# Transposed activations with 260-element rows in place of 256, and the warm-up tile in the `wide` buffer

## The reference

```python
xn = rms_norm(x, pre_norm)                       # (256, 2048)
proj = xn @ w_in                                 # 25 chunks of 512 columns, and 12 of merge gates
ya = dilated_attention(rope(q), rope(k), v) * silu(gate_a)
yb = banded_window_attention(rope(q), rope(k), v, 128, sink) * silu(gate_b)
yc = hgrn2_bidirectional(c_q, f_fwd, f_bwd, c_i, c_gate, ...)
y = g0 * (ya @ w_branch_a) + g1 * (yb @ w_branch_b) + g2 * (yc @ w_branch_c)
x = x + rms_norm(y @ w_out, post_norm)
```

## Time and profile before

| | before |
|---|---|
| median of 3 runs | 2167.24 us (2167.20 to 2167.29) |
| profiled execution, first to last instruction | 2165.5 us |
| outside this span (median less span) | 1.8 us |
| PE busy | 2156.1 us (100%) |
| PEld busy (loads of the stationary operand) | 1806.1 us (83%) |
| DVE / ACT / POOL busy | 70% / 49% / 58% |
| matmuls, and loads | 10062 each |

### The profile page before, as it was taken

The page is one execution under the profiler, slowest core; times in us unless marked ns, Lnnn a source line. Parts: engine busy times, 40 slices in busy tenths (PEclk is TensorE's granted clock), DMA queues, the critical chain, the costliest instruction groups (busy, mean ns, idle before and its releaser), DMA issues.

```text
span 2165.5 us, 25788 instructions
## 1 busy us (share of the span) xinstructions
PE 2156.1 (100%) x10062; PEld 1806.1 (83%) x10062; DVE 1517.6 (70%) x2192; ACT 1062.6 (49%) x1040; POOL 1258.3 (58%) x583
## 2 busy tenths in 40 slices
PE   9999999999999999999999999999999999999998
PEld 8888888888888888888888888888888888888887
DVE  7872789888656785655388637898996566865653
ACT  6444344546556564434454434345466566544442
POOL 4455544436685767666544555444476857676664
PEclk9999999999999999999999999999999999999999
DMA  8555444444445444655565554454544444546554
GB/s 327 192 191 193 173 175 180 151 176 183 168 173 176 174 175 168 251 193 191 192 217 193 192 192 175 169 181 148 184 176 174 174 175 163 186 166 251 192 193 151
DMA packets 59752, 403.66 MB, mean 186 GB/s; under 512 B 6768, under 2 KB 6896, under 8 KB 12272
## 3 DMA queue, kind: packets, MB, share of 16 engines
q1 hardware_dynamic: 59488, 401.49, 51.1%
q10 hardware_dynamic: 144, 0.52, 0.1%
HBM read 397.80 MB, written 4.19 MB: 186 GB/s over the span
## 4 chain that ended last, share of the span: by engine, by line
PE 98%; DVE 1%; DMA 1%; issue 0%; ACT 0%; DVEq 0%; POOLq 0%; POOL 0%; ACTq 0%
PE acc L1260 91%; PE side L1260 7%; DMA raw<-w_stream 1%; DVE w_lo L470 0%; PE side L1427 0%; ACT w_hi L467 0%; PE side L412 0%; DVE wide L1020 0%; DVE arena L893 0%; DVEq L482 0%; ACT stage L633 0%; POOLq L482 0%; POOL small L616 0%; DVE warm L967 0%; DVE small L885 0%
## 5 line engine op out<-in xcount | busy, mean ns | idle before, releaser
L470 POOL TENSOR_TENSOR w_lo<-raw,w_hi 128x768 fp32r<-128x768 f32 x367 | 1035.5, 2822 | 866.7 <-ACT w_hi L467 855.8
L467 ACT ACTIVATE w_hi<-raw 128x2048 fp32r<-128x2048 f32 x366 | 701.1, 1916 | 957.5 <-PE acc L1260 929.8
L470 DVE TENSOR_TENSOR w_lo<-raw,w_hi 128x1280 fp32r<-128x1280 f32 (+1 forms) x371 | 598.0, 1613 | 545.5 <-ACT w_hi L467 542.8
L1260 PE MATMUL acc<-w_hi,xT_hi 128*128 128x512 f32 x2112 | 654.2, 393 | 0.1
L1260 PE MATMUL acc<-w_hi,xT_lo 128*128 128x512 f32 x2112 | 648.6, 390 | 0.0
L1260 PE MATMUL acc<-w_lo,xT_hi 128*128 128x512 f32 x2112 | 527.8, 392 | 0.0
L1260 PEld LDWEIGHTS acc<-w_hi,xT_lo 128*128 128x128 f32 x2112 | 396.7, 188 | 83.2 <-DVE xT_lo L431 0.2
L1260 PEld LDWEIGHTS acc<-w_hi,xT_hi 128*128 128x128 f32 x2112 | 393.1, 188 | 78.7 <-issue 0.3
L1260 PEld LDWEIGHTS acc<-w_lo,xT_hi 128*128 128x128 f32 x2112 | 392.6, 188 | 78.3
L930 DVE STREAM_TRANSPOSE arena<-stage 32x256 f32<-32x256 f32 (+1 forms) x480 | 204.9, 427 | 7.0
L1260 PEld LDWEIGHTS side<-arena 128*128 128x128 f32 x864 | 118.8, 192 | 9.8
(11 more groups left out here) (146 smaller groups left out, 1909.8 us busy)
## 6 DMA issues: line engine op xcount, KB each, us to landing
raw<-w_stream SPq DMA_DIRECT2D x366, 1024.0 KB, 4.8
x_out<-arena SPq DMA_DIRECT2D x16, 256.0 KB, 3.1
arena<-x_turned_in SPq DMA_DIRECT2D x4, 514.0 KB, 7.3
arena<-x_in SPq DMA_DIRECT2D x2, 1024.0 KB, 14.6
arena<-x_in SPq DMA_DIRECT2D x4, 512.0 KB, 6.2
wide<-post_in SPq DMA_DIRECT2D x2, 1024.0 KB, 7.6
arena<-x_out SPq DMA_DIRECT2D x4, 512.0 KB, 5.7
raw<-w_stream SPq DMA_DIRECT2D x3, 512.0 KB, 7.0
```

The source lines that it names most:

```text
L467: return act.activation(w_hi[:, g % ROUNDED, :], raw[:, g % LANDING, :], ACT.Copy)
L470: return eng.tensor_tensor(w_lo[:, g % LANDING, cols], raw[:, g % LANDING, cols], w_hi[:, g % ROUNDED, cols].bitcast(F32), ALU.subtract)
L1260: return pe.matmul(out, a, b, start=start, stop=stop)
```

## The change

The rows of `xT_hi` and `xT_lo` become 260 elements long. Only the first 256 of each are used, so row k now begins 1040 k bytes after the buffer's start, in place of 1024 k. `SHIFT` is 4 elements, 16 bytes. Each of the two buffers is 256 bytes longer, so `xT_lo` begins 256 bytes further on and what is allocated behind it (`aT`, `bT`, `stage`, `wide`, `const` and others) 512 bytes further on. The tile `warm` loses its own 512 bytes and becomes the first 128 columns of `wide`. `raw`, `w_lo`, `w_hi` and everything in `arena` (`xP`, `yT`, `cT` too) stay where they were. No instruction is added, removed or moved on any engine, and no semaphore or wait changes.

```diff
 SPLIT = 1280
+SHIFT = 4
 PIECE = D // 4
...
         w_hi = sb("w_hi", [P, ROUNDED, TILE], F32R)
-        xT_hi = sb("xT_hi", [P, KT, T], F32R)
-        xT_lo = sb("xT_lo", [P, KT, T], F32R)
+        xT_hi = sb("xT_hi", [P, KT, T + SHIFT], F32R)[:, :, 0:T]
+        xT_lo = sb("xT_lo", [P, KT, T + SHIFT], F32R)[:, :, 0:T]
         aT_hi = sb("aT_hi", [P, 4, T], F32R)
...
         half_neg = sb("half_neg", [P, 1])
-        warm = sb("warm", [P, P])
+        warm = wide[:, 0:P]
```

## The result

The changed kernel takes 2196.84 us (2196.71 to 2197.05, 4 runs) beside 2167.26 us of the kernel before in the same session: ratio 1.0135, 95% interval 1.0123 to 1.0148, 29.6 us slower. The range of the prediction ended at 2174.

What follows compares the result with a forecast made beforehand. TensorE's chain of matmul distances was taken as the bound. Every part of the change was put at 0, so span 2165.5 + 0 and 1.8 us around it gave 2167.2 us, range 2160 to 2174.

Steps and rivals of the forecast that it cites:

- What bounds the kernel: Whole kernel: TensorE is 98% of the chain, so time is the sum of distances between matmuls; 226.7 ns on `xT`.
- The price list: The 6336 matmuls on `xT`: 1 ns on each is 6.3 us, or 0.29% of the time.
- The address of the loads: Loads of `xT` as stationary operand: 5940 of 6336 start at another place within 512 bytes; cost taken as 0.
- Reading (a): Large matmuls: whole kilobytes and 512-byte halves do not matter, all 226.7 to 227 ns; a clash depends on place within 512 bytes.
- Reading (b): Load against moving stream: a shifted start leaves the number of meetings within 512 bytes the same, unless only the first read counts.
- Reading (c): Window and dilated attention matmuls: the extra 11 ns go with the moving operand, 216 ns for 1024 bytes, 0.23 us over 2048.
- Reading (d): Turned score tiles: stationary operands with odd starts show nothing, mean 273 ns against 272 ns at multiples of 512.
- The slack of 38.7 ns: Loads on `xT`: a load takes 188 ns under a distance of 226.7, so a longer load is covered.
- -10.7 to +23.5 ns: Cost per shifted load: lower bound 226.7 less 216, upper bound one eighth of a 188 ns load; 0 taken.
- Rival B: Shifted loads: read in blocks wider than 16 bytes, 1.34 ns on 4752 loads, 6.4 us slower, 2173.6 us; chance 0.08.
- Rival A: Matmuls on `xT`: equal starts within 512 bytes make the 32 cycles, a shift removes them, 63.6 us, 2103.6 us; chance 0.13.
- C: Whole change: the address has no effect on anything, so the time is the forecast's; chance 0.79 together with the forecast.

Runs made afterwards that it cites:

- micro_b: No kernel work, TensorE alone: blocks of 96 fp32r matmuls, each behind eight plain fp32 products; rows of 256 elements 226.9 ns, rows of 260 231.6 ns.
- lo_rows: Kernel before with the warm-up tile in `wide` and only `xT_lo` in rows of 260, `xT_hi` unmoved: 2188.20 us, ratio 1.0094.
- micro_c: TensorE alone: blocks of 40 matmuls with 512 to 256 moving columns, then 256 pairs of stationary offsets; none under 226.7 ns, mean 231.6.
- micro_a: TensorE alone: blocks of 96 fp32r matmuls, each with its own operand starts; all loads 4 bytes further 232.3 ns, 8 bytes 230.7 ns.
- warm_only: Kernel before with only the warm-up tile moved into `wide`, `xT` keeping rows of 256: 2167.45 us, ratio 1.000.
- const256: Kernel before with the warm-up tile in `wide` and all of `xT` 256 bytes further on, rows of 256: 2167.34 us, ratio 1.0000.
- const240: Kernel before with the warm-up tile in `wide` and all of `xT` 240 bytes further on, rows of 256: 2170.64 us, ratio 1.0014.
- const16: Kernel before with the warm-up tile in `wide` and all of `xT` 16 bytes further on, rows of 256: 2193.58 us, ratio 1.0118.

## Why the prediction was wrong, point by point

**What bounds the kernel** held: TensorE's chain, 6336 matmuls on `xT`, 226.7 ns before. The price list too: 4.7 ns on each is the 29.6 us.

**The address of the loads** is the step that failed, by its value of 0. Reading (a), that whole kilobytes and 512-byte halves don't matter, held, and so did its conclusion that a clash could depend only on the place within 512 bytes (it is 256). Reading (b) is wrong. It counted meetings of load and stream and took their number for the cost. The runs show that the distance depends on where the two starts stand to each other: at offset 0 all distances in a block of `micro_b` but the first few are 226 or 227 ns; off it single distances go from 224 to 241 ns and most means lie between 228 and 237, and two of the offsets have two states. In place of the 0 a matmul on `xT` pays 4.7 ns on average, and `lo_rows` shows that one with an unmoved load pays too. The equal start of all operands was the one case in which the count said nothing, and it was the only case that the trace of before contained.

Reading (c) was half right. The 32 cycles don't shrink with a narrower load (`micro_b`), but `micro_c` shows that they don't go with the length of the moving operand either, as rows 7 and 8 had seemed to say. Reading (d) could not answer the question. Its loads with odd starts belong to plain fp32 products, in which 256 columns take 216 ns, about the time of 512 fp32r columns, so the moving operand comes at half the rate. It was no evidence for a stream at full rate, and in the fp32r stream of `micro_a` 4 and 8 bytes do cost, 5.6 and 4.0 ns.

The slack of 38.7 ns was a misreading too, since the recorded times of loads overlap. The trace of before had it beside rows 9, in the loads of the turned score tiles and a single load:

```profile
388.85 1.02 PEld L1427 LDWEIGHTS side<-const,wide 128*128 128x128 f32 x8
389.84 0.19 PEld L1260 LDWEIGHTS side<-arena 128*128 128x128 f32 x1
```

Eight loads of 0.19 us fit into 1.02 us. So 226.7 less 188 is no idle time in which a longer load hides.

The bounds themselves, -10.7 to +23.5 ns, held the 4.7 ns. The range did not, because its upper end was B's price, 1.34 ns from one invented block size. The text called (b) its weakest place but saw only a gain in its failing, and the upper bound was never turned into a time: 5940 x 23.5 ns would be 140 us. The 4.7 ns could not be read from the trace of before, which has no fp32r load off a multiple of 512 bytes.

**Rival B** had the right sign, the wrong size (6.4 us against 29.6) and the wrong mechanism. By it 64-byte steps are free, but rows of 272 cost 231.3 ns and a constant 64 bytes 233.2. **Rival A** did not happen: of the offsets tried none is faster than equal starts. **C** is refuted by the result.

**Writers and readers of `xT`, buffers further on, the warm-up tile**, each at 0, held: line 706's copies take 1124 ns after and 1120 before, and `warm_only` and `const256` run as the kernel before.

**The two cited rules.** The Trainium skill's "TensorE: Matmul & The Clock Gate", step-by-step part, says that loading the next tile doesn't take read bandwidth from the running matmul. In bf16 the trace shows nothing against it, 216 ns at all three offsets. For fp32r the place of the load alone moves the distance from 226.7 to as much as 234.2 ns; whether that is read bandwidth no run shows, but a cost of 0 did not follow from the rule. The Trainium skill's "SBUF — State Buffer", specifications table, gives a penalty for each cross to a new 16-byte line. From it the prediction concluded that shifts by whole lines cost 0, and those shifts are what costs; the 4 and 8 bytes of `micro_a`, which split lines, cost no more. The measurements decide in both.

**What stays open** is the mechanism: why the pattern repeats after 256 bytes, why moving one operand on is only roughly the same as moving the other back, what the states are, and why narrow loads are worse. Why every fp32r matmul of 512 columns has 32 cycles more than its columns, and bf16 about 6, is open too.

## What to carry to other kernels

Where a stream of fp32r matmuls with a load each bounds a kernel, let both operands' tiles start at multiples of 256 bytes, and pad rows only by whole 256 bytes: 16 bytes here cost 1.35% of the time. Some other pairs of offsets are as fast in blocks by themselves, none is faster, and an offset with two states isn't one to rely on. When all instances in a trace share one alignment, the trace says nothing of any other; a bound for leaving it should be priced in full, or measured first with a block of matmuls by themselves. For the change such a block gave the kernel's distance within 0.3 ns; for `lo_rows` and `const240` its forecast was 6 to 7 us too high, in `const240` because part of the kernel ran at 226.7 ns. And a row is evidence for a stream only if it runs at the same rate.

## What the runs showed of the hardware

- fp32r matmuls of 128 x 512 with a load each: 226.7 ns apart (544 cycles) when both operands start at multiples of 256 bytes, on average 231.6 ns over 256 pairs of offsets (seven at 226.7, none below, the worst 236.7). With 32-column loads 32 bytes off it is 239.2. The recorded time of a full load stays 188 ns.
- An unmoved load among moved ones pays as well: 229.2 ns in the `w_lo` passes of `lo_rows`.
- Offsets of 16 and 240 bytes have two states: `const16` 226.8 and 233.3 ns, `const240` 226.7 and 228.3, kept over many steps.
- bf16 matmuls of 128 x 512: 216 ns apart at all three offsets tried.
- Fewer moving columns save their cycles but not the 32 extra ones: 256 columns are 120 ns apart with a full load each, whose recorded time is 188 ns or a little more, so recorded loads overlap.
